# Bias rows read back skewed from 128 copies in DRAM, in a three-layer hybrid attention block

## The chip, the cores and the metric

The kernel runs on one core of one Trainium2 chip. The metric is the device time of one execution in microseconds (us). The engines are TensorE (PE, whose weight loads are shown as PEld), VectorE (DVE), ScalarE (ACT), GpSimd (POOL) and SyncE (SP). DMAs can be issued from SP, ACT and POOL.

## The reference, cut to what matters

Two layers (`L` = 0 and 1) of a hybrid attention block over 256 tokens of width 1024, then a third layer of another kind (`L` = 2). Of layers 0 and 1 the change touches how the relative position bias comes about, and the order of one reciprocal root:

```
proj = x @ w_in                                       # 256 x 2336
# groups A (6 heads) and B (4 heads, two score matrices each): scores with a relative bias
bias = bias_tab[t5_bucket(rel)]                       # depends on q - k only, per head
s = (q @ k.T) * scale + bias                          # then causal mask, softmax, @ v
# group C (6 heads): queries and keys from normed latents
q = rms_norm(c_q, q_norm_g) @ w_uq ; kv = rms_norm(c_kv, kv_norm_g) @ w_ukv
```

The same `rel_bias` (32 buckets x 10 heads) serves both layers, so the bias tiles are made once, in layer 0.

## The kernel before, in words

Each engine has its own program, written out by hand; semaphores join them. The order of a mixer (the attention half of a layer) is a list of stages made by `mixer_order(L)` (L192 to L295), which PE, ACT and DVE all walk. Around the change it is:

- Stages `win`: the product with `w_in`. Its weights come in 12 loads (column blocks 0 to 5, each in an upper and a lower half). They are called half-blocks 0 to 11 here; half-block 7 is the lower half of block 3. SP issues them (L887) into 3 raw buffers, each issue waiting until DVE has split the one three before. Every half-block is split by ACT into a rounded high part (`wh`, L1530) and by DVE into the rest (`wl`, L1784), and PE multiplies high and low parts (L1019 to L1021).
- Stage `vectors` (layer 0 only): small vectors are turned by PE, and PE multiplies `relb` (34 x 10, the bias table and two mask rows) with `hot` (34 x 384, one-hot buckets), L1193. DVE scales it to `brow`, 10 partitions x 384 (L2077), and signals `ev("brow")` with a small copy (L2079).
- Stages `latent_sums`, `latents`, `c`: DVE sums squares of the latents (L2101 to L2104), POOL takes the root `rs` (`power`, L2446), DVE scales the latents to `z` (L2111), PE turns them (L1217), ACT copies them to `cT` (L1577), and `uq` and `ukv` multiply them (L1229, L1239).
- Stage `ab`: PE turns queries and keys (L1206). Stage `ct`: the same for group C (L1251).
- Stages `flip` 0 to 4 (layer 0 only), then `S2`: scores of two heads (L1124), which DVE masks with `bias` in `masked` (L2019) and ACT exponentiates (L1554).

POOL's program around it (L2419 to L2460): 26 small DMA issues, 4 memsets, two loads for `uq` and `ukv` (`lnb` as `lora`), then the bias: wait for `brow`, write `bias_dram` (10 x 384), wait for that to land, issue the read into `bias`, and only then the latents' root:

```
gp.dma_start(bias_dram, brow[:, :]).then_inc(s_bias_out, 16)
gp.wait_ge(s_bias_out, 16)
gp.dma_start(bias[:, :, :], bass.AP(..., [[1, P], [384, A_H + B_H], [1, S]])).then_inc(s_bias_in, 16)
for L in range(DEPTH):
    power(rs[:, :, 0:2], va[:, :, 0:2], ev("var_lat", L), 1, ev("rstd_lat", L))
```

Partition p so holds row[p + n], while the scores need row[127 - p + n]. `flip_bias` (L1254) reverses the partitions: five products with a reversed identity `cv("flip")`, 128 x 512 each in two passes, that ACT (3) and DVE (2) copy back into `bias`.

PSUM has 8 banks of 512 columns; `plan()` fixes which bank each product takes, and `claim` waits until the bank's last product has been copied away. `hot`, `rowsA` and (before) `brow` lie in the buffer `cbuf`, which the latent products overwrite later, so `latent_keys` waits for the bias write (`s_bias_out`) on ACT and DVE.

Of the kernel before, what the change touches and what calls it, by code (L numbers as in the profile page):

```python
# [17 lines left out]
F32 = mybir.dt.float32  # L18
# [26 lines left out]
R2 = 16  # L45
NCMP = 15
TOPK = 64
SLOTW = 2048
# [21 lines left out]
def _const_layout():  # L70
    at = 0
    for name, n in (("ident", P), ("flip", P), ("causal", S), ("cos1", TT * 16), ("sin1", TT * 16), ("cos2", TT * 8),
                    ("sin2", TT * 8), ("cmpmask", TT * 16), ("cmpvalid", TT), ("cmpblock", 8), ("biasscale", 1)):
        CC[name] = (at, at + n)
        at += n
    return at
# [5 lines left out]
def constants():  # L82
# [7 lines left out]
    put("ident", np.eye(P))  # L90
    put("flip", np.eye(P)[::-1])
    put("causal", np.where(np.arange(S)[None] <= P + p, 0.0, NEG))
# [10 lines left out]
    put("cmpblock", (p // 32 == np.arange(8)[None] % 4) & (p // 16 % 2 == np.arange(8)[None] // 4))  # L103
    put("biasscale", np.where(p < A_H, 1 / SC_A, 1 / SC_B))
    d = 255 - np.arange(384)
# [86 lines left out]
def mixer_order(L):  # L192
# [43 lines left out]
    add(("wh", "win", 3, 1), *(("ct", n) for n in range(6)))  # L236
    if L == 0:
        add(*(("flip", n) for n in range(5)))
    def part(i, h, t, a=0, b=4):
# [164 lines left out]
def plan():  # L404
# [38 lines left out]
    def mixer(L):  # L443
# [6 lines left out]
        for stage, *a in ORDER[L]:  # L450
# [50 lines left out]
            elif stage == "ct":  # L501
                aside(("ct", L, a[0]), alt(a[0]))
            elif stage == "flip":
                aside(("flip", a[0]), alt(a[0]))
            elif stage == "S":
                put(("s", L, a[0]), 4, "dve")
            elif stage == "S2":
                put(("s", L, a[0]), 4, "dve")
                put(("s", L, a[0] + 1), SECOND[L].get(a[0] + 1, 0), "dve")
            elif stage == "wq" and (a[1], a[3]) == (1, 3):  # L510
                put(("win", L, a[0], a[2]), 2 * a[2] + a[0] % 2, alt(a[2]))
            elif stage == "T":
                put(("pt", L, a[0]), TURNED[L].get(a[0], 5), turns(L, a[0]))
            elif stage == "V" and JOBS[L][a[0]].last:
                g = JOBS[L][a[0]].group
                for t in range(TT):
                    put(("o", L, g, t), OBANK[L][g] + t, "dve", later=True)
            elif stage == "out" and a[1] < TT:
                empties.append(("o", L, a[0], a[1]))
            elif stage == "ht":  # L520
                put(("ht", L, a[0], a[1]), HT_BANK[L][a[0]][a[1]], "dve")
# [114 lines left out]
def program(nc, A, out):  # L636
    with ExitStack() as ctx:
# [6 lines left out]
        ps = ctx.enter_context(nc.psum_tensor("ps", [P, 8, 512], F32))  # L644
        bias_dram = nc.dram_tensor("bias_rows", [A_H + B_H, 384], F32, kind="Internal").ap()

# [30 lines left out]
        cbuf = at("cbuf", [P, TT, 1536])  # L677
        cT = at("cT", [P, 3, S])
        probs = at("probs", [P, 4, 384])
        pT = at("pT", [P, 2, 384])  # L680
# [14 lines left out]
        hot = at("hot", [34, 384], F32, cbuf_at + 1024)  # L695
        brow = at("brow", [A_H + B_H, 384], F32, cbuf_at + 1024 + 1536)
        lamin = at("lamin", [P, DEPTH, P], F32, cbuf_at + 4096)
# [7 lines left out]
        half = sb("half", [P, 8])  # L705
        relb = sb("relb", [34, A_H + B_H])
        mn = sb("mn", [P, 4, TT])
# [222 lines left out]
        def _(pe):  # L930
# [254 lines left out]
            def vectors():  # L1185
# [6 lines left out]
                pe.wait_ge(s_const, 16 * 3)  # L1192
                fill(mm(ps[0:A_H + B_H, b, 0:384], relb[:, :], hot[:, :], start=True, stop=True), ("relb",))  # L1193

# [46 lines left out]
            def turn_latent_heads(L, n):  # L1241
# [10 lines left out]
                fill(ins, ("ct", L, n))  # L1252

            def flip_bias(n):  # L1254

                pe.wait_ge(s_bias_in, 16)
                pe.wait_ge(s_cst, 32)
                b = claim(("flip", n))
                fill(mm(ps[:, b, :], cv("flip"), bias[:, 2 * n:2 * n + 2, :].rearrange("p h n -> p (h n)"), start=True, stop=True), ("flip", n))

# [166 lines left out]
            def mixer(L):  # L1427

                for stage, *a in ORDER[L]:
# [44 lines left out]
                    elif stage == "ct":  # L1474
                        turn_latent_heads(L, *a)
                    elif stage == "flip":
                        flip_bias(*a)
                    elif stage == "S":
# [38 lines left out]
        def _(act):  # L1517
# [68 lines left out]
            def latent_keys(L):  # L1586

                if L == 0:
                    act.wait_ge(s_bias_out, 16)
                for h in range(2):  # L1590
# [27 lines left out]
            def mixer(L):  # L1618

                for stage, *a in ORDER[L]:  # L1620
# [56 lines left out]
                    elif stage == "ct" and alt(a[0]) == "act":  # L1677
                        key = ("ct", L, a[0])
                        copy(ut[0:CQ, 10 + 2 * a[0]:12 + 2 * a[0], :], ps[0:CQ, U.bank[key], :].rearrange("p (c n) -> p c n", c=2), key)
                    elif stage == "flip" and alt(a[0]) == "act":  # L1680
                        key = ("flip", a[0])
                        copy(bias[:, 2 * a[0]:2 * a[0] + 2, :].rearrange("p h n -> p (h n)"), ps[:, U.bank[key], :], key)
                    elif stage == "S":
# [87 lines left out]
        def _(dve):  # L1771
# [241 lines left out]
            def masked(L, k):  # L2013

                j, key = JOBS[L][k], ("s", L, k)
                wait_full(dve, key)
                for t in range(TT):
# [42 lines left out]
            def vectors():  # L2060
# [15 lines left out]
                wait_full(dve, ("relb",))  # L2076
                me.empty(V.tensor_scalar(brow[:, :], ps[0:A_H + B_H, U.bank["relb",], 0:384], cv("biasscale")[0:A_H + B_H, :], None, ALU.mult), ("relb",))  # L2077
                me.settle()
# [35 lines left out]
            def latent_keys(L):  # L2114

                if L == 0:
                    dve.wait_ge(s_bias_out, 16)
                for h in range(2):
# [170 lines left out]
            def mixer(L):  # L2289

                pieces = {g: outputs(L, g) for g in range(len(GROUPS[L]))}
                for stage, *a in ORDER[L]:
# [76 lines left out]
                    elif stage == "ct" and alt(a[0]) == "dve":  # L2369
                        key = ("ct", L, a[0])  # L2370
                        copy(ut[0:CQ, 10 + 2 * a[0]:12 + 2 * a[0], :], ps[0:CQ, U.bank[key], :].rearrange("p (c n) -> p c n", c=2), key)
                    elif stage == "flip":
                        key = ("flip", a[0])
                        if alt(a[0]) == "dve":
                            copy(bias[:, 2 * a[0]:2 * a[0] + 2, :].rearrange("p h n -> p (h n)"), ps[:, U.bank[key], :], key)
                            me.settle()
                        else:
                            wait_done(dve, key)
                    elif stage == "S":
# [37 lines left out]
        def _(gp):  # L2417
            me = Steps(gp, pool_step)
            gp.dma_start(hot[:, :], A["hot"]).then_inc(s_const, 16)  # L2419
            gp.dma_start(relb[0:32, :], A["rel_bias"]).then_inc(s_const, 16)  # L2420
            gp.dma_start(relb[32:34, :], A["which"]).then_inc(s_const, 16)
            for rows, names, base in ((rowsA, ROWS_A, 0), (rowsB, ROWS_B, N_A)):
# [32 lines left out]
            gp.wait_ge(ev("brow"), 1)  # L2455
            gp.dma_start(bias_dram, brow[:, :]).then_inc(s_bias_out, 16)
            gp.wait_ge(s_bias_out, 16)
            gp.dma_start(bias[:, :, :], bass.AP(bias_dram.tensor, bias_dram.offset, [[1, P], [384, A_H + B_H], [1, S]])).then_inc(s_bias_in, 16)
            for L in range(DEPTH):
                power(rs[:, :, 0:2], va[:, :, 0:2], ev("var_lat", L), 1, ev("rstd_lat", L))  # L2460
                wait_full(gp, ("ukv", L, 1, 1))
                load_affine("ln1", L)
# [51 lines left out]
```

## Time and profile before

| | us |
|---|---|
| median of 3 runs | 1052.67 |
| lowest, highest | 1047.11, 1055.21 |
| the profiled execution | 1050.87 |
| its span, first to last instruction | 1049.0 |
| mean granted TensorE clock | 0.986 |

The three runs lie 8.1 us apart. The rows below come from one profiled execution; its span leaves 1.9 us around it. Times in rows are us from the start of the span. In a timeline or chain row the first number is the start and the second the duration; a bracket gives the idle time of the engine ahead of it and what ended it. Several instructions that follow one another on a line are merged ("x10").

### The profile page before, as it was taken

The page shows a single profiled execution, that of the slowest core. Times are in us where ns is not written, and L with a number is a line of the kernel's source. Part 1 is how long each engine was busy: PE and PEld are TensorE (multiplying, and loading weights), DVE is VectorE, ACT ScalarE, POOL GpSimd, SP SyncE. Part 2 cuts the span into 40 slices and gives each one's busy share as a digit, 9 for nine tenths or more (in the row PEclk, how much of TensorE's full clock was granted, in tenths as well). Part 3 has the DMA queues.
Part 4 walks back from the last instruction along what each step waited for, and adds up shares of the span by engine and source line. Part 5 has one row for each costly group of instructions (what it writes and reads, how often), then busy time and mean ns, then how long its engine had stood idle before and what let it go on. Part 6 is the DMA issues. An engine that isn't in the chain of part 4 may idle for free.

```text
span 1049.0 us, 14488 instructions
## 1 busy us (share of the span) xinstructions
PE 992.4 (95%) x5600; PEld 847.5 (81%) x5600; DVE 715.4 (68%) x1276; ACT 511.3 (49%) x897; POOL 47.9 (5%) x70
## 2 busy tenths in 40 slices
PE   6999989999999999998999999889988979999997
PEld 5878778888888898777888888788776768888886
DVE  3665677787886665677888787746777366666543
ACT  3455525555432346634555543345375265655531
POOL 5100020000000200011000000100000000000000
PEclk9999999999999999999999999989999989999999
DMA  8642429978694563245988776645221127666541
GB/s 290 212 140 81 121 60 301 262 221 269 212 360 137 158 191 121 82 121 162 293 242 253 257 294 229 186 148 161 82 79 42 41 68 214 186 177 198 192 171 40
DMA packets 191700, 184.97 MB, mean 176 GB/s; under 512 B 7131, under 2 KB 161014, under 8 KB 191633
## 3 DMA queue, kind: packets, MB, share of 16 engines
q1 hardware_dynamic: 188576, 175.85, 54.0%
q0 software_dynamic: 2768, 7.87, 2.5%
q8 instruction: 45, 0.74, 0.3%
q10 hardware_dynamic: 288, 0.33, 0.1%
q14 instruction: 23, 0.18, 0.1%
HBM read 182.97 MB, written 1.06 MB: 175 GB/s over the span
## 4 chain that ended last, share of the span: by engine, by line
PE 77%; DVE 12%; ACT 6%; issue 2%; POOL 1%; DMA 1%; SPq 0%; DVEq 0%; POOLq 0%; ACTq 0%
PE ps L1089 24%; PE ps L1041 15%; PE ps L1091 10%; DVE wl L1784 3%; PE ps L1019 3%; PE ps L1021 3%; PE ps L1020 3%; PE ps L1418 2%; ACT wh L1530 2%; PE ps L1124 2%; ACT probs L1554 2%; PE ps L1088 2%; PE ps L1177 1%; PE ps L1155 1%; PE ps L996 1%
## 5 line engine op out<-in xcount | busy, mean ns | idle before, releaser
L1089 PE MATMUL ps<-xhl,wh 128*128 128x512 f32 (+1 forms) x1040 | 359.2, 399 | 3.7 <-DVE xhl L1802 2.3
L1784 DVE TENSOR_TENSOR wl<-raw,wh 128x2048 fp32r<-128x2048 f32 (+5 forms) x140 | 303.5, 2170 | 84.2 <-ACT wh L1530 83.7
L1530 ACT ACTIVATE wh<-raw 128x2048 fp32r<-128x2048 f32 (+5 forms) x140 | 254.2, 1816 | 162.6 <-PE ps L1041 102.5
L1091 PE MATMUL ps<-xhl,wl 128*128 128x256 f32 (+1 forms) x910 | 255.2, 280 | 0.0
L1089 PEld LDWEIGHTS ps<-xhl,wh 128*128 128x128 f32 x1040 | 190.1, 191 | 38.6 <-DVE xhl L1802 2.6
L1091 PEld LDWEIGHTS ps<-xhl,wl 128*128 128x128 f32 x910 | 174.6, 192 | 5.2
L1717 ACT ACTIVATE scratch<-scratch 128x256 f32<-128x256 f32 x66 | 27.6, 418 | 144.1 <-DVE scratch L1875 144.1
L1875 DVE TENSOR_TENSOR scratch<-ps,scratch 128x256 f32<-128x256 f32 x132 | 55.7, 422 | 55.1 <-ACT scratch L1711 55.1
L1019 PE MATMUL ps<-wh,xhl 128*128 128x384 f32 (+4 forms) x204 | 74.9, 367 | 8.2 <-DVE xhl L1802 3.2
L1554 ACT ACTIVATE probs<-probs,mn 128x128 f32<-128x128 f32 (+1 forms) x128 | 56.7, 444 | 45.8 <-DVE mn L2019 45.7
L1041 PE MATMUL ps<-wh,gh 128*128 128x512 f32 x240 | 74.6, 392 | 0.0
L1041 PE MATMUL ps<-wl,gh 128*128 128x512 f32 x240 | 74.1, 390 | 0.0
L1041 PE MATMUL ps<-wh,gl 128*128 128x512 f32 x240 | 73.9, 389 | 0.0
L1020 PE MATMUL ps<-wl,xhl 128*128 128x384 f32 (+4 forms) x204 | 70.9, 347 | 0.0
L1021 PE MATMUL ps<-wh,xhl 128*128 128x384 f32 (+4 forms) x204 | 70.7, 347 | 0.0
L1865 DVE SCALAR_TENSOR_TENSOR adasum<-adaw,cact,adasum 128x512 f32<-128x512 f32 x84 | 62.9, 749 | 1.6
L1711 ACT ACTIVATE scratch<-ps 128x256 f32<-128x256 f32 x132 | 49.9, 378 | 23.4 <-PE ps L1089 22.8
L2446 POOL TENSOR_TENSOR rs<-va,half 128x1 f32<-128x1 f32 (+2 forms) x19 | 21.6, 1139 | 785.2 <-DVE va L1818 412.1
L1041 PEld LDWEIGHTS ps<-wl,gh 128*128 128x128 f32 x240 | 45.1, 188 | 9.6
L1041 PEld LDWEIGHTS ps<-wh,gl 128*128 128x128 f32 x240 | 45.1, 188 | 9.5
L1041 PEld LDWEIGHTS ps<-wh,gh 128*128 128x128 f32 x240 | 44.6, 188 | 8.8
L1019 PEld LDWEIGHTS ps<-wh,xhl 128*128 128x128 f32 x204 | 39.4, 193 | 13.5 <-issue 7.7
(285 smaller groups left out, 1475.6 us busy)
## 6 DMA issues: line engine op xcount, KB each, us to landing
raw<-in_w_down SPq DMA_DIRECT2D x33, 1024.0 KB, 5.0
adaw<-in_w_ada SPq DMA_DIRECT2D x24, 1024.0 KB, 7.6
raw<-in_w_gate SPq DMA_DIRECT2D x44, 512.0 KB, 4.1
raw<-in_w_up SPq DMA_DIRECT2D x44, 512.0 KB, 5.5
raw<-in_w_gate_up SPq DMA_DIRECT2D x44, 512.0 KB, 5.2
raw<-in_w_in SPq DMA_DIRECT2D x12, 768.0 KB, 5.1
raw<-in_w_in SPq DMA_DIRECT2D x8, 1024.0 KB, 5.1
raw<-in_w_o SPq DMA_DIRECT2D x8, 1024.0 KB, 4.9
```

The source lines that it names most:

```text
L1019: mm(o, xh[:, 4 * h + k, xs], a[:, k, :], start=h == k == 0, stop=False)
L1020: mm(o, xh[:, 4 * h + k, xs], b[:, k, :], start=False, stop=False)
L1021: ins = mm(o, xl[:, 4 * h + k, xs], a[:, k, :], start=False, stop=h == 1 and k == 3)
L1041: ins = mm(ps[:, 2 * t + h, :], x3[:, k, xs], w3[:, k % 2, h * 512:(h + 1) * 512], start=k == 0 and w3 is a and x3 is sh, stop=k == nk - 1 ...
L1089: ins = mm(o, a[:, v, k, :], xhl[:, :, k, c], start=k == 0, stop=k == KC - 1)
L1091: mm(o[:, 0, :], b[:, v, k, :], xh[:, k, c], start=False, stop=False)
L1530: me.go(activation(halves(item)[0][:, 0:n], raw[:, ITEM[item] % NRAW, 0:n], ACT.Copy), wh_ready)
L1554: ins = activation(probs[:, k % 4, a:e], probs[:, k % 4, a:e], ACT.Exp, bias=mn[:, k % 4, t:t + 1], scale=-1.0, accum_out=sums[:, SUMS_AT[ ...
L1711: me.go(activation((gsilu, gated)[v][:, i % 4, :], ps[:, U.bank[key], S:2 * S], ACT.Copy), cross_ready)
L1784: me.go(V.tensor_tensor(lo[:, 0:n], raw[:, ITEM[item] % NRAW, 0:n], hi[:, 0:n].bitcast(F32), ALU.subtract), wl_ready)
L1865: me.go(V.scalar_tensor_tensor(out=o, in0=w, scalar=cact[:, k:k + 1], in1=o, op0=ALU.mult, op1=ALU.add), ada_summed if n == 3 else None)
L1875: me.empty(V.tensor_tensor(o, ps[:, U.bank[key], 0:S], o, ALU.add), key)
```

## The change

The bias table is loaded 8 times beside itself (`COPIES` = 8): `relb` is 34 x 80, the product gives 80 partitions, and `brow` is 80 x 384, now in the place of `probs` (free until the first masked scores). POOL writes `brow` to a DRAM tensor of 10 x 128 x 384 with 8 DMAs; each takes the 10 partitions of one copy and writes every row 16 times. The read then steps 383 elements per partition from element 127, so partition p gets row[127 - p + n] at once. The `flip` stages, their constant (128 of the columns of `cst`), products, copies and waits go. DVE waits for the read ahead of its first masked scores. On POOL the latents' root of layer 0 stands between the 8 writes and the wait for them and the read. ACT's wait in `latent_keys` is for `ev("brow")` instead of the write; DVE's goes.

```
-        bias_dram = nc.dram_tensor("bias_rows", [A_H + B_H, 384], F32, kind="Internal").ap()
+        bias_dram = nc.dram_tensor("bias_rows", [A_H + B_H, P, 384], F32, kind="Internal").ap()
...
-        brow = at("brow", [A_H + B_H, 384], F32, cbuf_at + 1024 + 1536)
+        brow = at("brow", [COPIES * (A_H + B_H), 384], F32, place[0])
...
-                fill(mm(ps[0:A_H + B_H, b, 0:384], relb[:, :], hot[:, :], start=True, stop=True), ("relb",))
+                fill(mm(ps[0:COPIES * (A_H + B_H), b, 0:384], relb[:, :], hot[:, :], start=True, stop=True), ("relb",))
...
-            def flip_bias(n):
-                pe.wait_ge(s_bias_in, 16)
-                pe.wait_ge(s_cst, 32)
-                b = claim(("flip", n))
-                fill(mm(ps[:, b, :], cv("flip"), bias[:, 2 * n:2 * n + 2, :]..., start=True, stop=True), ("flip", n))
...
+                if L == k == 0:
+                    dve.wait_ge(s_bias_in, 16)          # in masked(), ahead of wait_full(dve, key)
...
-            gp.dma_start(relb[0:32, :], A["rel_bias"]).then_inc(s_const, 16)
-            gp.dma_start(relb[32:34, :], A["which"]).then_inc(s_const, 16)
+            for rows, src in ((slice(0, 32), A["rel_bias"]), (slice(32, 34), A["which"])):
+                n = rows.stop - rows.start
+                gp.dma_start(relb[rows, :].rearrange("r (c h) -> r c h", c=COPIES), src.unsqueeze(1).broadcast_to([n, COPIES, A_H + B_H])).then_inc(s_const, 16)
...
-            gp.dma_start(bias_dram, brow[:, :]).then_inc(s_bias_out, 16)
-            gp.wait_ge(s_bias_out, 16)
-            gp.dma_start(bias[:, :, :], bass.AP(bias_dram.tensor, bias_dram.offset, [[1, P], [384, A_H + B_H], [1, S]])).then_inc(s_bias_in, 16)
+            n = P // COPIES
+            for c in range(COPIES):
+                rows = brow[c * (A_H + B_H):(c + 1) * (A_H + B_H), :]
+                gp.dma_start(bias_dram[:, c * n:(c + 1) * n, :], rows.unsqueeze(1).broadcast_to([A_H + B_H, n, 384])).then_inc(s_bias_out, 16)
             for L in range(DEPTH):
                 power(rs[:, :, 0:2], va[:, :, 0:2], ev("var_lat", L), 1, ev("rstd_lat", L))
+                if L == 0:
+                    gp.wait_ge(s_bias_out, 16 * COPIES)
+                    gp.dma_start(bias[:, :, :], bass.AP(bias_dram.tensor, bias_dram.offset + P - 1, [[383, P], [P * 384, A_H + B_H], [1, S]])).then_inc(s_bias_in, 16)
```

## Rows read from the trace of the kernel before

**Rows 1.** The page's first part: busy time and share of each engine.
```profile
PE 992.4 (95%) x5600; PEld 847.5 (81%) x5600; DVE 715.4 (68%) x1276; ACT 511.3 (49%) x897; POOL 47.9 (5%) x70
```
**Rows 2.** The chain of waits in layer 0: start, duration, engine, line.
```profile
59.98 2.77 PE ps L1251 x24
62.76 4.29 PE ps L1259 x10
67.05 0.86 PE ps L1124 x8
...
154.34 0.70 DVE xhl L1796
```
**Rows 3.** The same chain in layer 1.
```profile
392.75 2.77 PE ps L1251 x24
395.52 0.88 PE ps L1124 x8
...
482.84 0.70 DVE xhl L1796
```
**Rows 4.** The timeline of POOL, 13 to 52 us.
```profile
13.06 0.53 POOL L2430 DMA_DIRECT2D sg<-in_subln_g  x1
13.59 0.53 POOL L2431 DMA_DIRECT2D b2v<-in_cmp_b  x1
...
14.87 0.74 POOL L2450 DMA_DIRECT2D lnb<-in_w_uq  x1 [0.30 <-POOL half L2435]
...
30.66 0.53 POOL L2456 DMA_DIRECT2D bias_rows<-brow  x1 [14.50 <-DVE mn L2079]
33.44 0.98 POOL L2458 DMA_DIRECT2D bias<-bias_rows  x1 [2.24 <-DMA bias_rows<-brow]
34.51 1.06 POOL L2446 TENSOR_TENSOR rs<-va,half 128x4 f32<-128x4 f32 x1
51.06 0.62 POOL L2439 DMA_DIRECT2D lnb<-in_ln_g  x1 [15.49 <-PE ps L1239]
```
**Rows 5.** The timeline of DVE around the latents' root.
```profile
32.52 0.16 DVE L2104 TENSOR_SCALAR va<-va 128x2 f32<-128x2 f32 x1
32.58 1.75 DVE L1784 TENSOR_TENSOR wl<-raw,wh 128x1536 fp32r<-128x1536 f32 x1
35.61 1.01 DVE L2111 TENSOR_SCALAR z<-proj,rs 128x256 f32<-128x256 f32 x4 [1.27 <-POOL rs L2446]
```
**Rows 6.** The timeline of PE's weight loads at the turned latents.
```profile
36.67 0.64 PEld L1217 LDWEIGHTS ps<-cst,z 128*128 128x128 f32 x6 [0.22 <-DVE z L2111]
```
**Rows 7.** DMA issues of windows 34.2:34.8 and 30:36 and 1040:1049: KB each, us from issue to landing.
```profile
bias<-bias_rows POOLq DMA_DIRECT2D x1, 1280.0 KB, 8.3
raw<-in_w_in SPq DMA_DIRECT2D x1, 768.0 KB, 8.3
bias_rows<-brow POOLq DMA_DIRECT2D x1, 15.0 KB, 2.5
out<-x SPq DMA_DIRECT2D x2, 256.0 KB, 2.0
```
**Rows 8.** DMA queues: packets, MB, share of 16 engines; windows 1040:1049 and 11:14.
```profile
q1 hardware_dynamic: 288, 0.52, 15.5%
q0 software_dynamic: 255, 0.05, 9.0%
```
**Rows 9.** Windows of 2 us: busy by engine, clock, DMA share, GB/s.
```profile
32.00:34.00 2.00, 1.49 (x9) 1.17 (x7) 1.97 (x7) 0.47 (x1) 0.56 (x1) 1.00 0.17 60
34.00:36.00 2.00, 1.61 (x9) 1.61 (x10) 0.73 (x3) 1.01 (x1) 1.47 (x2) 1.00 0.32 111
36.00:38.00 2.00, 2.00 (x15) 1.78 (x14) 2.00 (x4) 0.64 (x2) 0.00 (x0) 1.00 0.96 295
```
**Rows 10.** The timeline of ACT: half-blocks 7 and 8, and the copies between.
```profile
42.79 1.49 ACT L1530 ACTIVATE wh<-raw 128x1536 fp32r<-128x1536 f32 x1 [4.22 <-DMA raw<-in_w_in]
44.18 0.99 ACT L1523 ACTIVATE cbuf<-ps 128x288 f32<-128x288 f32 x3
48.21 1.91 ACT L1530 ACTIVATE wh<-raw 128x2048 fp32r<-128x2048 f32 x1 [1.49 <-PE ps L1021]
```
**Rows 11.** The chain of waits: the turned queries, and the first loads.
```profile
3.06 10.63 DMA raw<-in_w_in
45.65 0.44 PE ps L1206 x4
```

More of the change, by code:

```diff
@@ L46 @@
 NCMP = 15
+COPIES = 8
 TOPK = 64
@@ L71, in _const_layout @@
     at = 0
-    for name, n in (("ident", P), ("flip", P), ("causal", S), ("cos1", TT * 16), ("sin1", TT * 16), ("cos2", TT * 8),
+    for name, n in (("ident", P), ("causal", S), ("cos1", TT * 16), ("sin1", TT * 16), ("cos2", TT * 8),
                     ("sin2", TT * 8), ("cmpmask", TT * 16), ("cmpvalid", TT), ("cmpblock", 8), ("biasscale", 1)):
@@ L90, in constants @@
     put("ident", np.eye(P))
-    put("flip", np.eye(P)[::-1])
     put("causal", np.where(np.arange(S)[None] <= P + p, 0.0, NEG))
@@ L103, in constants @@
     put("cmpblock", (p // 32 == np.arange(8)[None] % 4) & (p // 16 % 2 == np.arange(8)[None] // 4))
-    put("biasscale", np.where(p < A_H, 1 / SC_A, 1 / SC_B))
+    put("biasscale", np.where(p % (A_H + B_H) < A_H, 1 / SC_A, 1 / SC_B))
     d = 255 - np.arange(384)
@@ L236, in mixer_order @@
     add(("wh", "win", 3, 1), *(("ct", n) for n in range(6)))
-    if L == 0:
-        add(*(("flip", n) for n in range(5)))
     def part(i, h, t, a=0, b=4):
@@ L502, in mixer @@
                 aside(("ct", L, a[0]), alt(a[0]))
-            elif stage == "flip":
-                aside(("flip", a[0]), alt(a[0]))
             elif stage == "S":
@@ L705, in program @@
         half = sb("half", [P, 8])
-        relb = sb("relb", [34, A_H + B_H])
+        relb = sb("relb", [34, COPIES * (A_H + B_H)])
         mn = sb("mn", [P, 4, TT])
@@ L1252, in turn_latent_heads @@
                 fill(ins, ("ct", L, n))
-            def flip_bias(n):
-                pe.wait_ge(s_bias_in, 16)
-                pe.wait_ge(s_cst, 32)
-                b = claim(("flip", n))
-                fill(mm(ps[:, b, :], cv("flip"), bias[:, 2 * n:2 * n + 2, :].rearrange("p h n -> p (h n)"), start=True, stop=True), ("flip", n))
             def gain_rows():
@@ L1475, in mixer @@
                         turn_latent_heads(L, *a)
-                    elif stage == "flip":
-                        flip_bias(*a)
                     elif stage == "S":
@@ L1588, in latent_keys @@
                 if L == 0:
-                    act.wait_ge(s_bias_out, 16)
+                    act.wait_ge(ev("brow"), 1)
                 for h in range(2):
@@ L1679, in mixer @@
                         copy(ut[0:CQ, 10 + 2 * a[0]:12 + 2 * a[0], :], ps[0:CQ, U.bank[key], :].rearrange("p (c n) -> p c n", c=2), key)
-                    elif stage == "flip" and alt(a[0]) == "act":
-                        key = ("flip", a[0])
-                        copy(bias[:, 2 * a[0]:2 * a[0] + 2, :].rearrange("p h n -> p (h n)"), ps[:, U.bank[key], :], key)
                     elif stage == "S":
@@ L2076, in vectors @@
                 wait_full(dve, ("relb",))
-                me.empty(V.tensor_scalar(brow[:, :], ps[0:A_H + B_H, U.bank["relb",], 0:384], cv("biasscale")[0:A_H + B_H, :], None, ALU.mult), ("relb",))
+                me.empty(V.tensor_scalar(brow[:, :], ps[0:COPIES * (A_H + B_H), U.bank["relb",], 0:384], cv("biasscale")[0:COPIES * (A_H + B_H), :], None, ALU.mult), ("relb",))
                 me.settle()
@@ L2114, in latent_keys @@
             def latent_keys(L):
-                if L == 0:
-                    dve.wait_ge(s_bias_out, 16)
                 for h in range(2):
@@ L2371, in mixer @@
                         copy(ut[0:CQ, 10 + 2 * a[0]:12 + 2 * a[0], :], ps[0:CQ, U.bank[key], :].rearrange("p (c n) -> p c n", c=2), key)
[L2372 to L2378, printed above, removed]
                     elif stage == "S":
```

## The prediction

> **What bounds the kernel now.** I read the busy shares first, then the chain of waits around the lines that the diff touches, then the timelines of POOL, DVE and PE there, and last the DMA views, because the change swaps TensorE work for traffic. TensorE is busy 95% of the span and carries the chain; POOL is nearly idle [rows 1], so anything taken off TensorE counts in full, and POOL counts only where somebody waits for it. In layer 0 the chain runs through the turned group C heads, then the ten passes of the five flips, 62.76 to 67.05, then the first scores [rows 2]. The reader should see that no gap stands between them. The flips wait for nothing: the bias landed 20 us earlier (issued at 33.44, 8.3 us) [rows 4, 7]. They cost their own 4.29 us and no stall.
>
> Layer 1 is the control, for it has the same stages without flips. There the scores start the moment the turned heads end [rows 3]. From the start of the turned heads to the end of the last split of hidden columns ahead of the FFN (both chain rows) it is 154.34 - 59.98 = 94.36 us in layer 0 and 482.84 - 392.75 = 90.09 us in layer 1. The difference is 4.27 us, the flips' own time. So nothing behind them hides them, and nothing new shows up when they are missing.
>
> **The change part by part.**
>
> *Flips removed.* 4.27 us off the path. Their five copies on ACT and DVE lay beside TensorE and bring nothing more. **-4.27 us.**
>
> *Eight write issues ahead of the root.* Before, POOL starts the first issue at 30.66 and the root at 34.51: 0.53 for the write's issue, 2.24 waiting for it to land, 0.98 for the read's issue, 0.1 between [rows 4]. The root's input was ready at 32.68 [rows 5], so POOL's queue already set its start. DVE idles 1.27 us for it, and PE's turned latents wait 0.22 us for DVE [rows 6]. The slack is therefore nought: each us that the root comes later goes to TensorE, and the products behind it run without a gap. After, the root stands behind eight issues. What is one worth? A load of 128 pieces takes 0.53, one of 256 pieces (`w_uq`) 0.74, and the bias read, 1280 pieces, 0.98 [rows 4]. A write here has 10 x 16 = 160 pieces, nearest the 0.53 rows; I take 0.54, and 0.1 more for the first. 8 x 0.54 + 0.1 = 4.4 us, plus the 0.1 ahead of the root: it starts at 30.66 + 4.5 = 35.15 instead of 34.51. **+0.64 us.** Ends: 0.50 each gives +0.25; 0.98 each gives 7.84 + 0.1, start 38.6, +4.1. The root's own 1.06 stays, as DVE is idle then. Behind it POOL waits for the writes and issues the read; queued there are only the `ln1` loads, which came at 51.06 and serve rows near 140 us.
>
> *Traffic of the writes.* 8 x 160 x 1536 B = 1.97 MB instead of 15 KB. The nearest row of a store is the output's: 0.52 MB in 15.5% of 9 us, 373 GB/s [rows 8]. At that rate the writes need 5.3 us. The queues are nearly empty from 32 to 36 us (shares 0.17 and 0.32) and full from 36 on [rows 9]. Starting near 31.7, 1.3 MB is gone when half-block 7 (0.79 MB, issued 34.4) begins to move near 35.3. The other 0.65 MB shares the engines with it: both are through after 1.44/0.373 = 3.9 us, near 39.2, and land about 40. Before, half-block 7 shared with the read and landed at 42.7 [rows 7]. So the writes take the place of the read there and cost nothing, provided they run at store rate. **0 us.** Cover and its end: ACT starts the split of half-block 7 as soon as it lands, 42.79, and behind that split stand the copies of `uq`; the first has ended by 44.5, and PE's turned queries need its bank at 45.65 [rows 10, 11]. That is 1.1 us of slack, and the root's delay adds 0.64: beyond 44.4 each us of landing costs one us. No row shows a large store out of ten partitions. The 15 KB write took 2.5 us against 2.0 for 256 KB of output [rows 7]; if all of that 0.5 us were movement, sixteen times the pieces would be 8 us a write and 64 us for eight, the far upper end. I take the store rate, since the row with data moving is the nearer one, and keep slower rates as a rival.
>
> *The read* is issued once the writes have landed, near 40, instead of 33.44. With 1 us to issue and 8.3 us as before it lands near 49.5, while the first masked scores come at 62.76 + 0.86, about 63.6. Half-blocks 8 and 9 share with it now. Half-block 8's split started at 48.21 and waited for PE, not for a load [rows 10], and TensorE uses it only behind the scores. **0 us**, covered by 14 us. If that cover goes, DVE stands in `masked`, with the next split and all later masks behind it.
>
> *Start.* The wider `relb` adds 222 small pieces and 32 more for the mask rows, 254 in all, in a stretch where the chain waits for weights until 13.69 [rows 11]. Small packets of POOL's queue took 9.0% of 3 us on 16 engines for 255, 17 ns each [rows 8]: 254 x 17 ns / 16 = 0.27 us. The 65 KB of the flip constant no longer loaded give back 65.5/373 = 0.18 us. **+0.1 us** (ends -0.2 and +0.7). The 80-partition product and scaling stream the same 384 columns: 0. Both moved waits for `brow` pass 20 us late: 0.
>
> Sum: -4.27 + 0.64 + 0 + 0 + 0.1 = **-3.5 us**. The profiled execution, 1050.87 (span 1049.0 and 1.9 around it), would become 1047.4. The median of the runs shown is 1.8 us above it: 1052.67 - 3.5 = 1049.2.
>
> **A rule against the change.** The Trainium skill, page "SBUF — State Buffer", section on the DMA port swizzle, says that DMA bandwidth depends on how many of 16 ports the partitions reach, about 27 GB/s a port, and ten neighbouring partitions reach three. By it one write would take an estimated 3.6 us, and the eight, partly side by side, about 18 us. No row here tests it: the output's stores use 128 partitions. The sum would then come out as the first rival below.
>
> **The rivals.**
>
> 1. *The writes drain slowly and hold the loads* (slower than before). Place: half-block 7, issued while the writes stand in the same 16 engines, each of which serves both queues. For it: one write takes its data from 10 partitions only, and before, the read and half-block 7 visibly landed together, 8.3 us each [rows 7]. Against: half-block 7 may get its turns regardless. It decides where the landing passes 44.4; it eats the 3.5 us where it passes 47.9, that is where the writes take 16 us, a third of store rate. At a third to a quarter (16 to 21 us) the landing is 48 to 53, the stall 4 to 8.5, the result +0.5 to +5; middle +3: 1055.7.
> 2. *Each write issue costs as much as the read's did* (0.98): -4.27 + 4.1 + 0.1 = 0: 1052.7. For: the pieces are spread with a repeated source row, like nothing in the trace. Against: 160 pieces are near 128.
> 3. *The bias itself is late.* Writes beyond 22 us push the read's landing past 63.6; at the far end of 64 us, 31.7 + 64 + 9.3 = 105, DVE is 41 us late and the result is some +37: 1090.
>
> **How the numbers follow.** Forecast -3.5 us: chance 0.57. Rival 1: 0.28. Rival 2: 0.11. Rival 3: 0.04, half of it over 1%. 1% is 10.5 us, about what a measurement of this kernel can tell from no change. No case except the far end of rival 3 gets there. So within 1%: 0.95; slower 0.03; faster 0.02, for a median drawn from runs 8 us apart. The time is the forecast's 1049.2. Range: below, -4.3 + 0.25 - 0.2 is -4.2, and medians of such runs may stand 4 us lower: 1044.5. Above it takes in rival 2 and most of rival 1: 1056.5.
>
> **What would show it.** Right: no L1259 rows; first scores 3.5 us earlier, near 63.5; the root near 35.2; half-block 7's split at or before 43; no DVE wait for the bias; 90.1 us from turned heads to the FFN. Rival 1: ACT waits on `raw` past 44.4 and PE idles at L1206. Rival 2: POOL's write rows near 1 us. Rival 3: DVE's mask waits for `bias`. The prediction is wrong if TensorE idles between 36 and 63 us.

## The result, and the profile after

The changed kernel (below: after) took 1057.32 us (median of 7 runs, 1051.97 to 1060.28), the kernel before, beside it, 1050.66 (7 runs, 1047.11 to 1055.26). The ratio is 1.0058, 95% interval 1.0036 to 1.0081: slower by about 6 us. That is inside the 1% I gave as "same", but the sign is wrong and the time lies above the range. The profiled execution took 1057.32, its span 1055.5 against 1049.0, its mean granted clock 0.983 against 0.986.

The page's busy shares show the flips gone and TensorE no busier [rows 1]; POOL has gained 4.5 us of work.

```profile
PE 990.4 (94%) x5590; PEld 847.2 (80%) x5590; DVE 713.8 (68%) x1274; ACT 509.5 (48%) x894; POOL 52.4 (5%) x77
```

The chain of waits of after, 35 to 162 us (start, duration, engine, line), answers to [rows 2] and to the turned queries of [rows 11]. L1202 is the turned queries, L1247 the turned heads, L1120 the first scores.

```profile
35.12 15.91 DMA raw<-in_w_in
51.11 1.48 ACT wh L1517
52.59 0.31 ACT cbuf L1510
53.04 1.09 PE ps L1202 x4
54.12 0.32 PE ps L1015
...
57.87 2.58 PE ps L1235 x8
...
69.68 2.35 PE ps L1247 x20
72.06 0.60 ACT ut L1510
...
72.90 0.93 PE ps L1120 x8
```

The reader should see a DMA of 15.9 us in a chain that before held only TensorE and splits here. It is half-block 7's load: issued at 35.12, landed at 51.0; before it landed at 42.7. The flips are gone: no product stands between the turned heads and the scores. But the turned queries start 7.39 us later (53.04 against 45.65) and the first scores 5.85 us later (72.90 against 67.05).

POOL's timeline of after answers to [rows 4].

```profile
31.43 4.79 POOL L2437 DMA_DIRECT2D bias_rows<-brow  x8 [15.01 <-DVE mn L2065]
36.32 1.06 POOL L2424 TENSOR_TENSOR rs<-va,half 128x4 f32<-128x4 f32 x1
50.88 1.03 POOL L2442 DMA_DIRECT2D bias<-bias_rows  x1 [13.50 <-DMA bias_rows<-brow]
```

Eight issues take 4.79 us, 0.60 each. The last write landed at 50.88, 19.45 us after the first issue began.

TensorE's waits from 36 to 75 us in after (engine, line, what it waited for: total us, times, longest):

```profile
PE ps L1202 <- ACT cbuf L1510: 5.6, 1, 5.6
PE ps L1213 <- DVE z L2097: 1.0, 1, 1.0
PE ps L1120 <- ACT ut L1510: 0.4, 1, 0.4
```

ACT is named, but ACT itself had stood for the load. Its timeline of after answers to [rows 10]: 10.73 us of idle instead of 4.22, and the copy of `cbuf` that TensorE wants stands behind that split.

```profile
51.11 1.48 ACT L1517 ACTIVATE wh<-raw 128x1536 fp32r<-128x1536 f32 x1 [10.73 <-DMA raw<-in_w_in]
52.50 1.29 ACT L1510 ACTIVATE cbuf<-ps 128x288 f32<-128x288 f32 x4
```

Windows of after (the columns of [rows 9]) show the queues and the clock:

```profile
34.00:36.00 2.00, 1.16 (x7) 0.85 (x6) 1.09 (x1) 1.49 (x1) 2.00 (x4) 1.00 0.97 115
36.00:38.00 2.00, 1.50 (x9) 1.18 (x7) 0.58 (x3) 0.00 (x0) 1.28 (x2) 1.00 0.82 119
...
50.00:52.00 2.00, 0.00 (x0) 0.00 (x0) 0.00 (x0) 0.89 (x1) 1.03 (x1) 0.70 0.80 309
52.00:54.00 2.00, 0.96 (x5) 0.99 (x6) 1.37 (x1) 2.00 (x6) 0.00 (x0) 0.50 0.84 260
54.00:56.00 2.00, 2.00 (x8) 2.00 (x8) 0.39 (x1) 0.76 (x2) 0.00 (x0) 0.50 1.04 385
```

Two things stand here. The 16 DMA engines are 97% and 82% busy while they move 115 and 119 GB/s; before, 96% busy went with 295 GB/s [rows 9]. They are occupied but move little. And after TensorE's idle stretch the granted clock is 0.50, which is 1.2 GHz, until about 57.5; the twelve `w_in` passes there start 0.32 us apart instead of 0.17 to 0.18.

**The account, from before to after, at the first scores.** First weights landed and were split from 14.44 instead of 13.72, and by the scaling into `brow` (30.43 against 29.68 in the two chains) the lag is +0.75. POOL's first issue to the root's start takes 36.32 - 31.43 = 4.89 us instead of 34.51 - 30.66 = 3.85: +1.04. The wait for half-block 7: +5.6. These three make the 7.39 at the turned queries, to within rounding of the rows. From there to `ukv` (L1235) nothing is waited for, and it takes 57.87 - 53.04 = 4.83 us against 48.18 - 45.65 = 2.53 before, as the clock is half: +2.30 (0.65 on L1202 itself, the rest on the passes). A wait for ACT's last copy ahead of the scores: +0.44. Flips: -4.29. Sum: 0.75 + 1.04 + 5.6 + 2.30 + 0.44 - 4.29 = +5.84, measured +5.85. The end of the hidden columns' split stands at 160.30 against 154.34 [rows 2], +5.96, and layer 1's first scores at 401.68 against 395.52 [rows 3], +6.16. So nearly all of it arises before 73 us; some 0.7 us more is added by the end of the span (1055.5 against 1049.0, +6.5).

### The profile page after: what moved, and what is told of

It reads as the page before. It is cut to its first block, busy times and chain, and to the rows that moved or that the text cites. A ratio compares the mean times of both kernels' runs of the same rounds, so it can differ in the third digit from the quotient of the medians.

```text
span 1055.5 us, 14462 instructions
## 1 busy us (share of the span) xinstructions
PE 990.4 (94%) x5590; PEld 847.2 (80%) x5590; DVE 713.8 (68%) x1274; ACT 509.5 (48%) x894; POOL 52.4 (5%) x77
## 3 DMA queue, kind: packets, MB, share of 16 engines
q0 software_dynamic: 3632, 9.84, 3.5%
## 4 chain that ended last, share of the span: by engine, by line
PE 75%; DVE 12%; ACT 6%; DMA 3%; issue 2%; POOL 1%; SPq 0%; DVEq 0%; POOLq 0%; ACTq 0%
PE ps L1085 24%; PE ps L1037 15%; PE ps L1087 10%; DVE wl L1768 3%; PE ps L1015 3%; DMA raw<-in_w_in 3%; PE ps L1017 3%; PE ps L1016 3%; PE ps L1407 2%; ACT wh L1517 2%; PE ps L1120 2%; ACT probs L1541 2%; PE ps L1084 1%; PE ps L1173 1%; PE ps L1151 1%
## 5 line engine op out<-in xcount | busy, mean ns | idle before, releaser
L1037 PE MATMUL ps<-wh,gl 128*128 128x512 f32 x240 | 73.9, 389 | 0.0
```

The source lines that it names most:

```text
L1037: ins = mm(ps[:, 2 * t + h, :], x3[:, k, xs], w3[:, k % 2, h * 512:(h + 1) * 512], start=k == 0 and w3 is a and x3 is sh, stop=k == nk - 1 ...
```

## The experiments

Theories. **P, ports:** a write whose source is ten neighbouring partitions drains slowly whatever the engines could move, holds the engines' queues, and the load behind it lands late. **B, bytes:** 1.97 MB more in the queue is what costs, whatever partitions they come from. **O, other:** the later root or the wider table.

**One write from 80 partitions.** The table is loaded narrow and widened by POOL, copies of a head side by side, so that one DMA can take all 80 partitions. Same bytes, same pieces.

```
-            for c in range(COPIES):
-                rows = brow[c * (A_H + B_H):(c + 1) * (A_H + B_H), :]
-                gp.dma_start(bias_dram[:, c * n:(c + 1) * n, :], ...)
+            gp.dma_start(bias_dram.rearrange("h (c n) k -> (h c) n k", n=n), brow[:, :].unsqueeze(1).broadcast_to([COPIES * (A_H + B_H), n, 384]))...
```

> Edit: the table's copies stand head by head (80 partitions, 8 neighbours hold one head), so one DMA with 1280 pieces of 1536 B takes all 80 partitions at once in place of eight that take 10 each; the same 1.97 MB reach DRAM. The wide table is made on POOL from a 34 x 10 load. Theory (the eight writes are slow because each draws from 10 neighbouring partitions, and half-block 7 stands behind them): the write lands within 10 us of its issue instead of 19.4, half-block 7 before 44, no wait of TensorE at its turned queries (5.6 us in the changed kernel), TensorE at its fast clock throughout 36 to 60 us, first scores near 63, time 3 to 4 us under the kernel before. Rival (1.97 MB of small repeated pieces into DRAM are slow whatever partitions they come from): the write takes 15 us or more again, half-block 7 lands near 50, the time stays 5 to 7 us over before.

Measured: 1048.26 (12 runs), ratio 0.9973 (0.9952 to 0.9993). First scores at 64.23, 2.8 us sooner than before: the flips' gain comes through, less a remnant. The write's issue took 0.89, and it landed 11.3 us after its start, a little slower than expected. DMA issues of this kernel, 28 to 36.5 us (KB, us to landing), and TensorE's waits:

```profile
bias_rows<-brow POOLq DMA_DIRECT2D x1, 1920.0 KB, 11.0
```
```profile
PE ps L1204 <- ACT cbuf L1512: 1.2, 1, 1.2
PE ps L1121 <- ACT ut L1512: 0.4, 1, 0.4
```

The queues from 34 to 36 us, first of after and then of this kernel (packets, MB, share of 16 engines), show why:

```profile
q0 software_dynamic: 68, 0.23, 96.6%
```
```profile
q0 software_dynamic: 123, 0.57, 100.4%
```

Both fill the engines. One packet occupies its engine for 2 x 16 x 0.966 / 68 = 0.455 us in after and 2 x 16 x 1.004 / 123 = 0.261 us here, though it is larger here (4.6 KB against 3.4). With the same bytes 8.2 us of landing went away (19.45 to 11.3), so bytes alone (B) are out as the whole cause. They are not free either: half-block 7 still took 10.3 us, and TensorE waited 1.2 us where none was expected.

**The narrow table alone.** After, with only the widening moved to POOL; the eight writes as they were.

```
+            gp.dma_start(reln[0:32, :], A["rel_bias"])...   # likewise the mask rows
+            gp.tensor_copy(relb[:, :].rearrange("r (c h) -> r c h", c=COPIES), reln[:, :].unsqueeze(1).broadcast_to([34, COPIES, A_H + B_H]))...
```

> Edit: the changed kernel with the 34 x 10 table loaded as before and widened to 34 x 80 on POOL, eight writes of 10 neighbouring partitions kept. Theory: the 40-byte pieces of the wide load delay the first weights; without them the first scores of the trace, and the start of the eight writes, come 0.5 to 0.8 us earlier than in the changed kernel, and nothing else moves: the writes take 19 us, TensorE waits 5 to 6 us. Rival (the 0.75 us at the start is a difference between runs): the writes still start at 31.4.

Measured: 1055.53 in one run. First weights split at 13.63 and first scores at 70.19, while the writes landed 17.8 us after the first issue and TensorE waited 4.2 us. The start's 0.75 us comes back; the hold stays. The rest of the 2.7 us at the first scores is a wait shorter by 1.4 and less slow clock, more than expected; why the writes landed 1.7 us sooner than in after is open. The run also shows that the widening on POOL does not by itself lift the hold.

**The wide table alone**, in the kernel before.

> Edit: the kernel before with the bias table loaded 8 times beside itself (272 pieces of 40 B instead of 34); the product uses the first 10 columns, all else as before. Theory: half-block 2 lands near 14.4 instead of 13.7, and the first scores come 0.7 us later than 67.05. Rival (the 0.75 us of the changed kernel's trace was chance): half-block 2 lands at 13.5 to 13.8.

The edit is the diff's wide `relb` loads, with the product still reading ten columns. Measured: 1051.81 in one run. The chain of its first loads, and of its first scores:

```profile
3.12 12.68 DMA raw<-in_w_in
...
69.07 0.86 PE ps L1125 x8
```

Here the first weights landed at 15.8, 2.1 us later than before [rows 11], and the scores 2.0 us later. In after it was 0.75. Both are on the path one for one; why the same 238 extra pieces of 40 bytes (34 x 7; the prediction said 254) cost once 0.75 and once 2.1 is open.

**The writes' rows spread, and their order.** The kernel with one write, copies of a head side by side, but with eight writes again: write c takes partitions c, c + 8, ..., c + 72.

```
-                rows = brow[c * (A_H + B_H):(c + 1) * (A_H + B_H), :]
+                rows = brow[c::COPIES, :]
```

> Edit: as the changed kernel, eight writes of ten rows, but the ten partitions of one write lie 8 apart (0, 8, .. 72) instead of side by side. Wide table made on POOL. Same bytes, pieces, issues and ten rows per DMA. Theory (neighbouring partitions share a port): the eight writes are through in about half the time, 10 us instead of 19.4, half-block 7 lands near 43 to 45, TensorE waits 0 to 1 us at its turned queries. Rival (a DMA of ten rows runs on ten engines, and that is the limit): unchanged, 19 us, landing near 50, wait 5 to 6 us.

Measured: 1055.05 in one run; the writes landed 18.85 us after the first issue and TensorE waited 4.8 us. That missed: about half was expected. The next theory: taken write by write, rows eight apart reach more ports, but the first four writes reach the same ones, and so do the last four; the writes run side by side, so what would matter is what those in flight reach together. The next kernel has this one's writes in another order and nothing else:

```
-            for c in range(COPIES):
+            for c in (0, 4, 1, 5, 2, 6, 3, 7):
```

> Edit: the eight writes whose ten rows lie 8 partitions apart, issued in the order 0, 4, 1, 5, 2, 6, 3, 7 instead of 0 to 7. Nothing else differs from the run in order 0 to 7, whose writes had all landed 18.9 us after the first issue at 160 GB/s. 
> The spread rows with the writes in the order 0, 4, 1, 5, 2, 6, 3, 7, now timed beside the kernel before. In its single run the first scores came at 65.46. Shared ports: the shorter hold keeps the gain of the flips, ratio 0.996 to 1.000. If order does not matter (total bytes alone): as with the order 0 to 7, whose single run was 1055.05, ratio 1.002 to 1.006.

Measured: 1048.58 in the single run, and timed 1048.72 (10 runs, one of them an outlier at 2480 that the ratio leaves out), ratio 0.9985 (0.9964 to 1.0005), which is not clear of no change against the kernel before; the traces tell more. POOL's timeline, first of the order 0 to 7, then of the mixed order; the bracket of the read ends when the writes have landed:

```profile
30.46 4.83 POOL L2440 DMA_DIRECT2D bias_rows<-brow  x8 [13.59 <-DVE mn L2067]
...
49.31 1.03 POOL L2445 DMA_DIRECT2D bias<-bias_rows  x1 [12.86 <-DMA bias_rows<-brow]
```
```profile
30.62 4.83 POOL L2440 DMA_DIRECT2D bias_rows<-brow  x8 [13.58 <-DVE mn L2067]
...
45.20 1.03 POOL L2445 DMA_DIRECT2D bias<-bias_rows  x1 [8.59 <-DMA bias_rows<-brow]
```

**Decoy writes in the kernel before.** Flips kept, root kept; behind the root POOL issues the same 1.97 MB, from ten partitions at a time (eight writes) or from 80 at once (one), into a tensor that nobody reads.

```
+                    for c in range(8):
+                        gp.dma_start(decoy_dram[:, 16 * c:16 * c + 16, :], cst[10 * c:10 * c + 10, 0:384].unsqueeze(1).broadcast_to([10, 16, 384]))...
```

> Edit: the kernel before (flips kept, narrow table, root where it was) plus eight more writes on POOL right behind the latents' root, each 10 neighbouring partitions of constants 16 times into a tensor that nobody reads. No engine waits for them. Theory (slow writes in the shared engines hold the weights): half-block 7, issued 34.4, lands near 48 to 54 instead of 42.7, TensorE waits 4 to 9 us at its turned queries, its granted clock falls behind that wait, and the time is 6 to 11 us over before. Rival (what hurt was the later root, or the missing flips, not the traffic): no wait at the turned queries and the time within 1 us of before.

> Edit: as the run with eight decoy writes, but the same 1.97 MB go as one write of 80 partitions 16 times. Theory: at 285 GB/s instead of 120 the same bytes hold half-block 7 for 3 to 5 us at most; TensorE waits 0 to 4 us, time 0 to 4 us over before, at least 4 us under the eight writes. Rival (bytes, not the source's width, are what costs): the same as the eight writes, 6 to 11 us over.

Measured: ten at a time 1053.86 (10 runs), ratio 1.0040 (1.0015 to 1.0064); 80 at once 1056.15 (10 runs), ratio 1.0057 (1.0034 to 1.0081). Half-block 7 landed at 46.5 and at 47.5, first scores came at 71.58 and 72.68 against 67.05. Both expectations missed. The ten-partition writes cost about half of what I had for them (3.6 us of time against 6 to 11, a wait of 2.8 against 4 to 9). The second fell outright: I had it cheap, and it was no cheaper than the first. So these two kernels do not separate P from B. TensorE's waits, 36 to 66 us, of ten and of 80:

```profile
PE ps L1209 <- ACT cbuf L1526: 2.8, 1, 2.8
```
```profile
PE ps L1209 <- ACT cbuf L1526: 3.8, 1, 3.8
```

The queues from 42 to 46 us, of 80 at once:

```profile
q0 software_dynamic: 272, 1.25, 75.7%
q1 hardware_dynamic: 272, 0.42, 27.6%
```

The two queues moved as many packets each, 272 and 272, as if they took turns; with ten partitions at a time it was 335 and 328. POOL's packets are 4.6 KB here, the load's 1.5 KB, so the load gets a quarter of the bytes. In these kernels POOL's queue holds the bias read (1.31 MB) and the decoy (1.97 MB) together while half-block 7 moves; in the second half-block 7 took 13.1 us. So B is half right: enough bytes in POOL's queue hold a load too, from any partitions. By these rows the run with one write did better than this one also because its 1.97 MB were alone and were issued 3.7 us ahead of the load.

Even turns are not what held the load in after. Its queues from 38 to 42 us:

```profile
q0 software_dynamic: 171, 0.44, 86.2%
q1 hardware_dynamic: 106, 0.16, 10.8%
```

From 36 to 38 us it was 133 packets of POOL's against 1 of the load, from 38 to 40 us 65 against 29, from 40 to 42 us 106 against 77; in the first 7 us behind its issue half-block 7 (0.79 MB) moved 0.16 MB. In the kernel below that issues half-block 8 behind ten-partition writes the same stands, 155 packets against 3 from 40 to 42 us. In the decoy kernels the load was issued 1 us ahead of the writes, and there it got its turns. So in after the load fared worse than by turns; whether its place behind the writes makes that difference was not tested.

**The root's place.** In the kernel before, the root moved between the write and the wait for it, as the change has it, and nothing else.

> Edit: the kernel before with nothing but the order on POOL changed: the latents' root between the small write and the wait for it and the read. Flips and narrow table kept. Theory: the root's input is ready at 32.7 and DVE is splitting weights from 32.6 to 34.3, so a root that starts earlier takes longer (2.48 us against 1.06, as in layer 1 and in the run with 16 copies) and ends near 35.2 instead of 35.6; TensorE reaches the turned latents at 36.7 anyway, so the first scores move by 0 to 0.3 us and the time not at all. Rival (the root's place is worth its 1.8 us): first scores 1 us or more earlier.

Measured: 1050.49 in one run, before 1050.85 on the same chip; first scores at 67.22 against 67.05. POOL's timeline:

```profile
32.93 2.49 POOL L2446 TENSOR_TENSOR rs<-va,half 128x4 f32<-128x4 f32 x1 [1.56 <-DVE va L2104]
35.40 1.03 POOL L2461 DMA_DIRECT2D bias<-bias_rows  x1
```

The root starts 1.6 us sooner than in [rows 4] and takes 2.49 us instead of 1.06, so it ends at 35.42 against 35.57. The move alone is worth nothing that these rows show: started while DVE splits weights, the root takes longer by what it starts sooner.

**The root ahead of the eight writes.** The kernel with the narrow table, and only these two swapped.

```
+            power(rs[:, :, 0:2], va[:, :, 0:2], ev("var_lat", 0), 1, ev("rstd_lat", 0))
             for c in range(COPIES): ...
```

> Edit: the changed kernel with the narrow table widened on POOL, and the latents' root ahead of the eight writes of ten neighbouring rows instead of behind them. Theory: the root ends near 35.5, the 1 us wait of TensorE at the turned latents goes, but the writes start near 35.5 and still stand around half-block 7: it lands between 44 and 50, TensorE waits 1 to 5 us at its turned queries, and the read lands only a few us ahead of the first masks. First scores between 64 and 69. Rival (the late root was what pushed everything): no wait at the turned queries, first scores at 63.

> The kernel after with the narrow table and the root ahead of the eight writes, now timed beside the kernel before. In its single run the writes were issued at 35.20, behind half-block 7 (issued 34.3, landed 38.8), so that half-block 8 was the load held (16 us, TensorE idle 1.8 us, no slow clock) and the first scores came at 65.38, 1.7 us before those of before. If a hold costs only what its cover lacks: ratio 0.996 to 1.000. If the traffic of the writes costs the same wherever it lies: +5 us over the flips' gain, ratio 1.002 to 1.006.

Measured: 1048.27 in the single run, and timed 1048.13 (10 runs), ratio 0.9980 (0.9968 to 0.9992). POOL's timeline and the chain of the single run:

```profile
32.80 2.42 POOL L2425 TENSOR_TENSOR rs<-va,half 128x4 f32<-128x4 f32 x1 [15.74 <-DVE va L2092]
35.20 4.87 POOL L2441 DMA_DIRECT2D bias_rows<-brow  x8
...
53.73 0.98 POOL L2447 DMA_DIRECT2D bias<-bias_rows  x1 [13.66 <-DMA bias_rows<-brow]
```
```profile
37.96 16.06 DMA raw<-in_w_in
54.10 1.92 ACT wh L1519
...
65.38 0.86 PE ps L1121 x8
```

The writes are no faster: 18.5 us from first issue to landing. But half-block 7 is issued at 34.3, ahead of them, and lands in 4.5 us, where I had expected it to be held again; the load that is held, for 16 us, is half-block 8. TensorE needs what ACT does behind that split only later, and waits 1.8 us for it, at the full clock. The same slow traffic, 4.6 us later, costs 1.8 us of wait (1.2 in the timed kernel's profile) instead of 4.2 and a slow clock, and the first scores come 4.8 us sooner than with the narrow table alone (65.38 against 70.19). About 1 us of that is not the hold: TensorE's wait for the turned latents, 1.0 there, is gone with the earlier root. This separates the hold from its cover: a hold of the same length costs by which load stands behind it.

**Sixteen copies, eight reads.** The runs point to less store traffic. Here `brow` stays at ten partitions, one write makes 16 copies of each row (0.25 MB), and eight reads fill `bias`, each the partitions g, g + 8, ... with a step of 376 elements.

```
+            gp.dma_start(bias_dram, brow[:, :].unsqueeze(1).broadcast_to([A_H + B_H, 16, 384]))...
+                    for g in range(8):
+                        gp.dma_start(bias[g::8, :, :], bass.AP(bias_dram.tensor, bias_dram.offset + P - 1 - g, [[376, 16], [16 * 384, A_H + B_H], [1, S]]))...
```

> Edit: no wide table. One write of the 10 rows 16 times (0.25 MB, 160 pieces), then eight reads, each into 16 partitions that lie 8 apart. No flips; the root between the write and the wait for it. Theory: the write lands within 4 us of its issue, the root starts as soon as its input is ready, near 33 to 34.5, half-block 7 lands by 43, TensorE waits nowhere between 36 and 60 us, the reads land by 50, first scores near 62.8, time 4 us under before. Rival: eight reads into few partitions each hold half-block 8 or 9, or the skewed read itself is what is slow; then TensorE waits behind 45 us and the time is no better than before.

Measured: 1046.32 (12 runs), ratio 0.9956 (0.9938 to 0.9974), the fastest kernel of the study. Its POOL timeline, and its first scores in the chain:

```profile
30.61 0.64 POOL L2433 DMA_DIRECT2D bias_rows<-brow  x1 [14.43 <-DVE mn L2065]
32.70 2.48 POOL L2423 TENSOR_TENSOR rs<-va,half 128x4 f32<-128x4 f32 x1 [1.45 <-DVE va L2090]
36.35 4.31 POOL L2439 DMA_DIRECT2D bias<-bias_rows  x8 [1.17 <-DMA bias_rows<-brow]
```
```profile
63.06 0.93 PE ps L1120 x8
```

One ten-partition write of 240 KB lands after 5.5 us (within 4 was expected), and POOL, done with the root, waits 1.2 us for it; the eight reads are issued behind it, half-block 7 is never waited for, and the scores come 4.0 us sooner than before. The flips' 4.27 us are real, and this is the kernel that collects them: 4.45 us less at the medians (1050.77 before, beside it).

## Why the prediction was wrong, point by point

- **Flips removed, -4.27: right.** 4.29 in the account; with sixteen copies the scores come 3.99 us sooner; there, too, TensorE waits 0.5 us for ACT's last copy, which the flips had hidden. I had concluded from layer 1 that nothing new would show up; this small wait did.
- **Traffic of the writes, 0 us: this step failed.** I wrote "I take the store rate, since the row with data moving is the nearer one" and had the writes through near 39.2. They landed at 50.88, and half-block 7 at 51.0 instead of 40. The row I took stores from 128 partitions; after drained 115 GB/s from 34 to 36 us, 80 partitions at once 283, and neither reached the 373 I used. Every row I had of a store from ten partitions was the 15 KB one, and I called it the farther. That the load would share the engines evenly with them was wrong as well: it got 107 of 411 packets from 36 to 42 us. The cost is 5.6 us of wait plus 2.30 of slow clock, 7.9 us.
- **The cover was right.** I had 1.1 us of slack and then one for one beyond 44.4; a landing at 51.0 gives 6.6 by that, with my 0.64 for the root and 0.1 for the start 7.34 at the turned queries, where 7.39 was measured.
- **Issues ahead of the root, +0.64: low.** 0.60 an issue instead of 0.54 made it +1.04. A line through 128 pieces (0.53) and 256 (0.74) puts 160 at 0.58; I had taken the 128 row. (The ends I gave, +0.25 and +4.1, count only one of the two 0.1 us of the forecast; with both they are +0.35 and +4.2.)
- **Start, +0.1: low.** +0.75 in after, beyond even the upper end of 0.7. I priced small pieces by their time in the queues (and 254 of them, where it is 238); the first weights landed later by more than that.
- **The read, 0 us: right, with less to spare.** It was issued at 50.88 instead of 40 and took 9.3 us; the first masks came at 73.9 and waited for TensorE alone. Part of that cover is luck: the hold that delayed the read delayed the scores too.
- **The clock: not priced.** I had written that TensorE's idling would show me wrong, but gave the idling no second price.
- **Rival 1 was what happened**, in place and size: a landing of 48 to 53 and 16 to 21 us of writes (19.45 measured), a stall of 4 to 8.5 us. Its result of +0.5 to +5 lacked the clock, so after stood at +6. I left it at 0.28 because no row tested it. Rivals 2 and 3 did not occur. The Trainium skill, page "SBUF — State Buffer", section on the DMA port swizzle, had put the writes at an estimated 18 us, inside this rival's 16 to 21; I cited it and did not follow it.

Left open: why the wide table costs 0.75 us here and 2.1 there, why the load in after got fewer turns than in the decoy kernels, and the slow clock's cause as such. No run made TensorE idle without the traffic; what the traces have in common stands below.

## What to carry to other kernels

A DMA's rate is read from a row with the same side of the transfer: how many partitions, and which. If the only store rows use 128, take the slow end as the forecast for a store of ten. Then ask which load stands behind it in the engines: swapping one small operation ahead of the writes moved the hold to a load that was needed later and brought the first scores from 70.19 to 65.38, without moving a byte less. (The times, 1055.53 in a single run and 1048.13, differ by more, but runs of one kernel here lie up to 8 us apart.) And when a table can be made wider by writing or by reading, let the reads do it: sixteen copies in DRAM and eight reads needed 0.25 MB of stores instead of 1.97.

## What the runs showed of the hardware

- **Stores from few partitions occupy the engines.** They were 97% busy at 115 GB/s in after; a packet held its engine 0.455 us against 0.261 us from 80 partitions. The order of otherwise equal writes changed the whole from 18.85 to 14.6 us.
- **POOL's queue and SP's moved as many packets each** where the load was issued ahead of the stores (272 and 272, 335 and 328). The one with the longer packets gets the bytes: 1.25 MB against 0.42. Behind stores of ten partitions a load got far fewer packets: 107 of 411 (after, 36 to 42 us), 3 of 158 (root ahead, 40 to 42 us).
- **The clock fell behind the longer of these idle times.** TensorE idle for 5.6, 4.8, 4.2, 3.8 and 2.8 us (after, the spread rows, the narrow table, the two decoys) was followed each time by windows at a granted 0.50, and the `w_in` passes started 0.32 us apart instead of 0.17; idle of 1.8, 1.2 and 1.1 us was not. So a wait there costs more than its length: 2.30 us on top of 5.6 in after.
- **POOL's root took 1.06 us with DVE idle and 2.42 to 2.49 us with DVE splitting weights**, in the four kernels where it started that soon; in the kernel before, moving it sooner into a split brought nothing.
